# A two-block transformer kernel: the seven-product weights' sums made in DRAM, and the conditioning and the mixer's first panels dealt out anew

## The reference, cut to what matters

```python
x = x + fox_mixer(rms_norm(x), ...)                  # 16 heads, causal, forget gates
x = x + square(relu(rms_norm(x) @ w_up)) @ w_down    # "ff_a", hidden width 4096
x = x + mla_mixer(rms_norm(x), ...)                  # 8 heads, low-rank queries and keys
x = x + square(relu(rms_norm(x) @ w_up)) @ w_down    # "ff_b"
x = rms_norm(x, final_norm_g)
mod = silu(c) @ ada_w + ada_b                        # "conditioning": 6 vectors of 1024
h = rms_norm_2(x, tm_pre_g) * (1 + sc_t) + sh_t
x = x + g_t * rms_norm_2(token_mixer(h, ...), tm_post_g)
x = x + g_c * rms_norm_2(conv_ffn(...), cm_post_g)
```

## Time and profile before

| | us |
|---|---|
| median of 3 runs | 1982.04 |
| lowest and highest of them | 1981.69, 1982.6 |
| the profiled execution, its own time | 1981.71 |
| its span, first to last instruction | 1980.0 |

### The profile page before, as it was taken

The page is one execution under the profiler, slowest core; times in us unless marked ns, Lnnn a source line. Parts: engine busy times, 40 slices in busy tenths (PEclk is TensorE's granted clock), DMA queues, the critical chain, the costliest instruction groups (busy, mean ns, idle before and its releaser), DMA issues.

```text
span 1980.0 us, 29280 instructions
## 1 busy us (share of the span) xinstructions
PE 1961.3 (99%) x10404; PEld 1640.2 (83%) x10404; DVE 1341.7 (68%) x2145; ACT 894.3 (45%) x1417; POOL 60.4 (3%) x114
## 2 busy tenths in 40 slices
PE   9999999999999999999999999999999999999999
PEld 7777789898987887898988788778888888888888
DVE  6555579687777776797787769574444686563545
ACT  4555554445444554544444443474333544432333
POOL 0000000000110110000001100000000000000000
PEclk9999999999999999999999999999999999999999
DMA  4332243323562114523226513211322412223232
GB/s 158 86 85 85 75 148 129 106 79 98 184 205 78 52 49 157 179 69 106 96 99 214 190 46 104 74 64 65 96 96 98 151 43 85 96 95 105 88 99 91
DMA packets 61292, 209.05 MB, mean 106 GB/s; under 512 B 7160, under 2 KB 10232, under 8 KB 61200
## 3 DMA queue, kind: packets, MB, share of 16 engines
q1 hardware_dynamic: 49920, 168.32, 25.8%
q0 software_dynamic: 10560, 37.28, 6.0%
q10 hardware_dynamic: 720, 2.23, 0.3%
HBM read 205.66 MB, written 2.13 MB: 105 GB/s over the span
## 4 chain that ended last, share of the span: by engine, by line
PE 94%; DVE 4%; ACT 1%; DMA 1%; issue 1%; SPq 0%; DVEq 0%; ACTq 0%
PE bank L893 23%; PE bank L895 23%; PE bank L894 23%; PE bank L1216 4%; PE bank L1218 4%; PE bank L1217 4%; PE bank L1016 1%; PE bank L1091 1%; PE bank L1075 1%; PE bank L998 1%; PE bank L1001 1%; PE bank L1043 1%; PE bank L949 1%; PE bank L951 1%; PE bank L950 1%
## 5 line engine op out<-in xcount | busy, mean ns | idle before, releaser
L893 PE MATMUL bank<-b_hi,w_hi 128*128 128x512 f32 x2060 | 813.0, 395 | 6.6 <-DVE w_lo L2764 4.0
L895 PE MATMUL bank<-b_hi,w_lo 128*128 128x512 f32 x2060 | 802.9, 390 | 0.0
L894 PE MATMUL bank<-b_lo,w_hi 128*128 128x512 f32 x2060 | 802.7, 390 | 0.0
L893 PEld LDWEIGHTS bank<-b_hi,w_hi 128*128 128x128 f32 x2060 | 387.2, 188 | 95.9 <-issue 8.2
L895 PEld LDWEIGHTS bank<-b_hi,w_lo 128*128 128x128 f32 x2060 | 387.0, 188 | 81.0
L894 PEld LDWEIGHTS bank<-b_lo,w_hi 128*128 128x128 f32 x2060 | 387.4, 188 | 80.2 <-issue 2.4
L2764 DVE TENSOR_TENSOR w_lo<-w_raw,w_hi 128x1024 fp32r<-128x1024 f32 (+3 forms) x259 | 306.8, 1185 | 210.2 <-ACT w_hi L1810 209.5
L1810 ACT ACTIVATE w_hi<-w_raw 128x1024 fp32r<-128x1024 f32 (+3 forms) x259 | 265.5, 1025 | 263.3 <-PE bank L895 253.6
L3916 DVE SCALAR_TENSOR_TENSOR arena<-bank,vec,arena 128x511 f32<-128x511 f32 x88 | 65.7, 749 | 85.8 <-ACT arena L2658 80.5
L1216 PE MATMUL bank<-parts,w_hi 128*128 128x256 f32 x384 | 108.7, 283 | 3.3 <-DVE x L3113 3.3
L1218 PE MATMUL bank<-parts,w_lo 128*128 128x256 f32 x384 | 107.9, 281 | 0.0
(11 more groups left out here) (398 smaller groups left out, 2537.9 us busy)
## 6 DMA issues: line engine op xcount, KB each, us to landing
w_raw<-in_wstream SPq DMA_DIRECT2D x253, 512.0 KB, 3.5
arena<-in_ada POOLq DMA_DIRECT2D x48, 512.0 KB, 4.3
plain<-in_wseven SPq DMA_DIRECT2D x24, 512.0 KB, 5.0
early<-in_wseven SPq DMA_DIRECT2D x24, 512.0 KB, 6.8
w_raw<-in_wstream SPq DMA_DIRECT2D x12, 384.0 KB, 3.0
arena<-crow POOLq DMA_DIRECT2D x16, 256.0 KB, 4.8
w_raw<-in_wstream SPq DMA_DIRECT2D x10, 256.0 KB, 2.6
x<-in_xT ACTq DMA_DIRECT2D x4, 512.0 KB, 6.6
```

What stands on the lines that cost most here:

```text
L893: nc.tensor.matmul(dst, whi, rhs_hi(k), start=(k == 0), stop=False)
L894: nc.tensor.matmul(dst, whi, rhs_lo(k), start=False, stop=False)
L895: last = nc.tensor.matmul(dst, wlo, rhs_hi(k), start=False, stop=(k == n - 1))
```

## The change

1. The four sums of each unit are made in DRAM, in a new tensor `seven_sums`, by POOL's DMAs. For a group of two units (256 rows of 2048 floats) four transfers follow each other: copy all (2 MB); add the second and third pieces onto the first two of the four column blocks (1 MB); add twice more (512 KB each). `sum_turn(turn)` waits for all transfers of the turns before and issues the four steps for four different groups. There are 12 groups and 15 turns: turns 0 to 8 behind the row loads of the first attention, turn 9 at its end, turn 10 after ff_a's conditioning, turns 11 to 14 between POOL's subtractions in the second. The copies and sums are written in rows of 1 KB (`r (a c) -> r a c`, c = T // 2); in the built program the pieces that lie side by side are one access again: 32 x 16384 floats for the copy, 256 x 1024 and 256 x 512 for the sums.
2. SP loads each of the seven blocks by itself (128x512, 256 KB), into a ring of eight; a pair of loads waits until the pair eight before it is split. DVE's `two`, `three` and `four` are gone.
3. The conditioning: 6 steps early in ff_a, 9 in its last up tiles, 6 in its last segment as before; then only 3 in `mla_out`, from its fourth tile on, where the wait for the row now stands; 18 in ff_b's chunks (in up tiles 2, 4 and 6 of each, and after steps 11, 18 and 25 of its products), through one new buffer in `plain` and `early`; one in each of its last six up tiles; none in its last segment.
4. The splits of the mixer's three panels go one by one into ff_b's last segment, after the second, fourth and sixth tile's split; that segment is written out, with other places for the panels' splits.

```diff
+            def sum_turn(turn):
+
+                pool.wait_ge(sum_in, sum_count(turn))
+                for back, (to, src, at) in enumerate(((slice(0, 4 * T), seven_rows, slice(0, 4 * T)),
+                                                      (slice(0, 2 * T), seven_rows, slice(T, 3 * T)),
+                                                      (slice(2 * T, 3 * T), sum_rows, slice(0, T)),
+                                                      (slice(3 * T, 4 * T), sum_rows, slice(2 * T, 3 * T)))):
+                    if 0 <= turn - back < SUM_GROUPS["ff_b"]:
...
+                            pool.dma_start(dst, src, accum_op=ALU.add).then_inc(sum_in, 16)
...
-            with pool.Fori(1, FOX_PAIRS // 2) as pp:
-                for m in range(2):
-
-                    pool.wait_ge(row_min, 12 * pp + (6 * m - 6))
-                    rows(2 * pp + m, m)
+            sum_turn(0)
+            for p in range(2, FOX_PAIRS):
+
+                pool.wait_ge(row_min, 6 * p - 6)
+                rows(p, p % 2)
+                sum_turn(p - 1)
+            for turn in range(FOX_PAIRS - 1, FOX_PAIRS + 1):
+                sum_turn(turn)
 
             pool.wait_ge(ctx_lo, FOX_PAIRS)
             pool.dma_start(ada_at[1][1], d["cvec"].to_broadcast([P, D])).then_inc(ada_cin, 16)
+            sum_turn(FOX_PAIRS + 1)
...
+                if i >= SEVEN_RING and i % GROUP == 0:
+                    sp.wait_ge(seven_lo, seven_count(i - SEVEN_RING + GROUP - 1))
...
+            def chunk_condition(c, i):
+
+                if i % SEVEN == 4 and i >= SEVEN:
+                    k = ADA_MORE + 2 * ADA_CHUNK * c + ADA_CHUNK + i // SEVEN - 1
+                    conditioning(k, k % 2, 2)
...
-                        if i % SEVEN == 0:
-                            four(at // SEVEN)
-                        if i % SEVEN == 2 and i + 5 < end:
-                            two(at // SEVEN + 1)
-                        if i % SEVEN == 4 and i + 3 < end:
-                            three(at // SEVEN + 1)
+                        if run == "ff_b":
+                            chunk_condition(c, i)
```

ACT's end of ff_b:

```diff
-                def last_square(j):
-                    square(j)
-                    if run == "ff_b":
-                        for p in range(MIX_W):
-                            mix_split(p)
-
-                segment(run, first + n, KT, last_mid, nothing, lambda: last_square(j), fresh=1)
+                square(j)
+                w_split(first + n + 1)
+                for k in range(2, KT):
+                    w_split(first + n + k)
+                    last_mid(k - 2, k % 2)
+                    if k % 2 == 0:
+                        mix_split(k // 2 - 1)
+                last_mid(KT - 2, 0)
```

More of the change, by code:

```diff
@@ L373, in program, with seven_raw @@
         ff_s = [ar(8), ar(9)]
[L377 to L384 removed]
+        SEVEN_RING = 8
+        GROUP = 2
+        N_GROUPS = SEVEN_RING // GROUP
+        PIECE = (0, None, None, 3, None, None, 2)
+        SUM_AT = (None, 1, 2, None, 0, 3, None)
+        UNITS = QUAD * SEVEN_CHUNKS
+        def seven_raw(i):
+            r = i % SEVEN_RING
+            return (plain if r < SEVEN_RING // 2 else early)[:, 2 + r % (SEVEN_RING // 2), :]
         def seven_count(i):
@@ L683, in program, with sum_count @@
         wflat = d["wstream"]
-        def seven_src(n):
-            size = 4 * P * T
-            return d["wseven"][n * size:(n + 1) * size].rearrange("(p c) -> p c", p=P)
+        seven_rows = d["wseven"].rearrange("(r c) -> r c", c=4 * T)
+        sum_rows = nc.dram_tensor("seven_sums", (2 * UNITS * P, 4 * T), F32, kind="Internal").ap()
+        def sum_count(turn):
+            return 16 + 16 * sum(min(max(turn - back, 0), SUM_GROUPS["ff_b"]) for back in range(4))
         block = ctx.enter_context(nc.Block())
@@ L740, in load_ffn @@
                         sp.wait_ge(free, count)
+                        sp.wait_ge(sum_in, sum_count(SUM_GROUPS[run] + 3))
                     if c < SEVEN_CHUNKS:
-                        for q in range(QUAD):
-                            load_seven(QUAD * seven_chunk(run, c) + q)
+                        end = SEVEN * QUAD
+                        for i in range(end):
+                            load_seven(end * seven_chunk(run, c) + i)
                 load_panels(at, KT)
@@ L860, in _ @@
                 pool.dma_start(dst, d[name]).then_inc(const2_in, 16)
-            condition(ADA_B + ADA_UP + 2, 6 * KT, 1)
             pool.wait_ge(ada_done, 6 * KT)
@@ L2150, in seven_ffn @@
                 j = first + n - 1
-                def last_square(j):
-                    square(j)
-                    if run == "ff_b":
-                        for p in range(MIX_W):
-                            mix_split(p)
-                segment(run, first + n, KT, last_mid, nothing, lambda: last_square(j), fresh=1)
+                if run == "ff_a":
+                    segment(run, first + n, KT, last_mid, nothing, lambda: square(j), fresh=1)
+                    return last_mid
+                square(j)
[6 more added lines that the diff above has]
+                last_mid(KT - 2, 0)
                 return last_mid
@@ L3166, in up_tiles @@
                         else:
-                            n0 = QUAD * seven_chunk(run, c)
-                            two(n0)
-                            low(SEVEN * n0)
-                            low(SEVEN * n0 + 1)
-                            three(n0)
+                            low(SEVEN * QUAD * seven_chunk(run, c))
+                            low(SEVEN * QUAD * seven_chunk(run, c) + 1)
                         if not last:
@@ L3246, in lead1 @@
                         dve.sem_inc(x_sum, 2)
-                        mix_splits()
-                segment(run, last + 1, KT, last_add, last_post, lead0, lead1)
+                if run == "ff_a":
+                    segment(run, last + 1, KT, last_add, last_post, lead0, lead1)
+                    return last_add, last_post
+                w_split(last + 1)
+                lead0()
+                w_split(last + 2)
+                lead1()
+                last_add(0, 0)
+                for k in range(2, KT):
+                    w_split(last + 1 + k)
+                    last_add(k - 1, (k - 1) % 2)
+                    last_post(k - 2, k % 2)
+                    if k % 2 == 0:
+                        mix_low(k // 2 - 1)
                 return last_add, last_post
```

152 lines of the change are left out of this document (80 added, 72 removed).

## The result

The changed kernel takes 2005.26 us (median of four runs), the kernel before 1981.87: ratio 1.0116, 95% interval 1.0104 to 1.0129. It is 23 us slower, where 1974.2 us had been forecast and the range ended at 1981.5. The profiled execution spans 2002.6 us, that of before 1980.0.

The account below looks back on a forecast made before the run. PE was taken as the bound, busy 1961.3 of 1980.0 us. Terms 3.24 + 1.79 + 2.88 + 1.7 - 0.5 - 1.35 = 7.8 us off 1981.71 gave 1973.9, as median 1974.2; range 1971.0 to 1981.5.

Parts of the forecast that it names:

- X: Time of one turn of the DRAM sums on POOL's queue: taken as 20 us, bounds 10 and 43.
- the point of decision: First attention: turns up to about 25 us cost nothing; above 25.6 each further us delays DVE's first conditioning step 8.75 us.
- counting the added part twice: In a turn's time: an add's target is read too, so 6.3 MB and 15 us instead of 10.
- Rival (c): Turns don't fit POOL's queue in the first attention, delaying conditioning and PE; 1989 us at 28 us a turn; chance 0.17.
- the cover of a panel: First attention: a panel's load issued at 141.89 was used at 164.04, so 22 us from issue to use.
- the second attention was harmless: Second attention: POOL's subtractions stand ahead of the turns they could meet, or have 13 us.
- four starts of the fast product: Chunks 0 and 1 of both feed-forwards: PE's four 0.81 us stalls behind DVE's adds go, winning 3.24 us.
- second attention's output: Moving the row's wait to the fourth tile brings DVE's work earlier; both PE stalls go, winning 1.79 us.
- ff_b's end, wait and clock: ff_b's last segment: the 2.88 us stall goes with mixer panels one by one, and 1.7 us of low clock.
- chunk ends, three: Conditioning step after step 25 stands between half panels in the chunks: new stall of 0.45 us, three times, 1.35 us.
- last hidden rest: ff_b's end: DVE's last hidden rest comes after the second mixer panel's rest, a new PE stall of 0.5 us.
- ring of 256 KB loads: SP's seven 256 KB transfers a unit: cost 0; upper end 2 us beyond the cover at nine places.

Follow-up runs that it names:

- Run 9: Changed kernel with each adding transfer made a plain copy of the same shape and bytes, so sums are wrong; 1984.9 us, ratio 1.0008 to the kernel before.
- run 8: Changed kernel with turn 9 moved from ahead of the store of silu(c) to ahead of turn 10; 1990.1 us, ratio 1.0043 to the kernel before.
- run 1: Changed kernel without the sums in DRAM, SP loading raw weight pieces of the same bytes instead; 1971.5 us, ratio 0.9949 to the kernel before.
- run 5: Changed kernel with the 256x1024 add issued as two adds of 256x512 in rows of 2 KB; 2008.1 us, ratio 1.0135 to the kernel before.
- run 6: Changed kernel with the 2 MB copy issued as two transfers in rows of 4 KB; 2014.3 us, ratio 1.0165 to the kernel before.
- run 2: Changed kernel with the 256x1024 add in rows of 2 KB, as one transfer; 2348.4 us, ratio 1.1845 to the kernel before.

## Why the prediction was wrong

**The step that failed first: a turn's time.** The prediction took X = 20 us, "by the nearest rows, those of large transfers", between 10 and 43, and put the point of decision at 25.6. Run 9 shows that 20 us is what copying costs (19.6 to 22.0), and adding brings it to 27. The prediction's own sum had 15 us for moving alone (10 + 5) and 5 for counting the added part twice. So of the 7 us missed, 5 lie in the rate of moving and only 2 in adding: counting the added part twice was the right kind of step. That the added part's target is read too, its reason, no view shows: the pages of the changed kernel and of run 9 both have 275.39 MB read from HBM. What shows is the time. A packet of 4 KB takes 0.33 us when added (246 to 262 us of the changed kernel) and 0.16 when copied (240 to 257 us of run 9; medians). The 418 GB/s of the earlier trace rows is a rate of loads into SBUF, and the copy of 2.1 MB, landing after 9.9 us (median), ran at 211 GB/s, about half of it. No row showed such a transfer, and 5.6 us between the chosen value and the point of decision was too little to give the case 0.17.

**Rival (c) was the right mechanism for the larger single loss.** Its turns "end at 52 + 8.75 X": turn 1 went out at 51.91 and turn 9's last transfer landed at 297.0, which is X = 28.0. For that it had priced 21 us for DVE and 15 for PE; DVE's first step was 20.6 us late and run 8 got 15.2 us back by moving one turn. Its time of 1989 was still 16 us short, since it held nothing of the panels.

**The step that failed second: the cover of a panel.** The prediction read "a panel whose load was issued at 141.89 was used at 164.04, 22 us later". That pairs two rows which don't belong together. Panels go through two buffers, so the load of 141.89 fills the one that DVE has just left, and its use is two splits on. ACT of the kernel before:

```profile
154.46 1.06 ACT L1810 ACTIVATE w_hi<-w_raw 128x1024 fp32r<-128x1024 f32 x1
```

The cover was 12.6 us, and 9 after landing. In the dense segments it is far less. SP and ACT of before, at the end of ff_a:

```profile
601.95 6.29 SPq L707 DMA_DIRECT2D w_raw<-in_wstream  x2
```
```profile
607.72 1.06 ACT L1810 ACTIVATE w_hi<-w_raw 128x1024 fp32r<-128x1024 f32 x1 [2.22 <-PE bank L895]
```

5.8 us from issue to use, 2.3 after landing at 605.5, one of the shortest. Along the kernel before the slack after landing is mostly 7 to 12 us in the first attention until 235, mostly 3 to 5 from 240 on and in the dense segments, mostly 7 to 12 in the second attention from 655 on. The prediction used one number for all of them, and the wrong one.

**And the landing.** The sum has no term for what a turn does to the landing of SP's panels; all that stood against it was the cover above. A panel took 11.6 and 12.4 us, more than three times its 3.5, for it stood still at first (2.9 us of the load of 247.88), and beside the add it then moved slowly (5.2). Up to 715 us this was worth 17 us in the changed kernel and 17.7 in run 8, more than the 14 to 15 of the queue that rival (c) spoke of, and it stood in no rival at all. The claim that the second attention was harmless fell with it: it lost 7.1 us at 680.

**The parts that were right.** What the other parts did is read from run 1 against the kernel before, by the matmuls' twins:

| term | forecast, us | measured, us |
| --- | --- | --- |
| four starts of the fast product | -3.24 | -5.4 |
| second attention's output | -1.79 | -2.4 |
| ff_b's end, wait and clock | -2.88 - 1.7 | -4.65 |
| chunk ends, three | +1.35 | +2.0 |
| last hidden rest | +0.5 | +0.4 |
| ring of 256 KB loads | 0 | 0 |
| the rest | 0 | -0.2 |
| sum | -7.8 | -10.2 |

The mechanisms all held; the short waits were priced low by one common error. A wait costs more than its idle time. The first matmuls after the 1.39 us wait of the changed kernel:

```profile
286.34 0.49 PE L929 MATMUL bank<-b_hi,w_hi 128*128 128x512 f32 x1 [1.39 <-DVE w_lo L2802]
286.68 0.40 PE L930 MATMUL bank<-b_lo,w_hi 128*128 128x512 f32 x1
```

0.34 us from start to start, where 0.23 is usual: 0.1 us. The other part lies ahead of the wait. Idle time is counted from the end of the last matmul, which stands 0.39 us behind its start, while the next would have started after 0.23: 0.16 us. So here 1.39 + 0.16 + 0.10 = 1.65 us were lost, and at a start of the fast product 0.81 + 0.16 + 0.07 = 1.04. There 0.3 more came bit by bit within the same chunk, which is not explained.

## What to carry to other kernels

A background transfer had two prices here: its own time, some 27 us a turn, and what it did to the landing of the other queue's loads while it ran, up to 14.6 us in place of 3.5. Before one is added, list the slack of each load stretch by stretch, pairing a load with its use through the buffer it fills (with two buffers, the second use on), and put the transfers where slack is larger than the delay, cut small enough for that. And nothing that someone waits for, however small, goes into a queue behind a bulk transfer: here 4 KB landed after 22.6 us in place of 1.6.

## What the runs showed of the hardware

- A copy from DRAM to DRAM of 2 MB lands 8.3 to 11.6 us after its issue (the first one 13.2). Behind it an accumulating transfer of 1 MB takes 11.1 us where a copied one takes 6.7 (medians); in rows of 2 KB (run 5) it takes 11.7.
- A panel's load of 512 KB issued by SP beside the first stages of a turn starts its first packet 3.8 to 6.1 us after the issue in the changed kernel, in place of 0.95, and lands after 11.6 to 14.6 us in place of 3.5. POOL's packets moved meanwhile were copying ones of 64 KB or adding ones of 4 KB (changed kernel), or copying ones of 4 KB (run 6: first packet after 4.8 us). After that both queues move packets, 238 of POOL's and 229 of SP's from 252 to 262 us.
- A transfer whose outermost dimension was 2 took the time of 2.1 engines of 16 (13.2%): 0.88 MB in 36 us (run 2).
- PE's clock around five waits of the changed kernel: full all through after 2.0 us of idleness at 260 and 1.4 at 285 (but in run 9 half for 3.4 us after 1.8 us at 256); half (PEclk 0.50) for 3.4 us after 3.6 us at 617, for 6.8 us from 3.3 us into the 5.0 at 680, for 13.7 us from 2.4 us into the 12.4 at 292.
